# Interleaving VectorE's convolution taps of two chunks, with a third buffer and a later gate load, in an encoder trunk on one Trainium2 core

## The reference, cut to what matters

```python
def conformer_conv_module(h, w_in, b_in, w_dw, b_dw, ln_g, ln_b, w_out, b_out):
    D = h.shape[-1]
    u = h @ w_in + b_in
    u = u[..., :D] * jax.nn.sigmoid(u[..., D:])
    u = lax.conv_general_dilated(
        u, w_dw[:, None, :].astype(u.dtype),
        window_strides=(1,), padding=[(CONV_WIDTH - 1, 0)],
        dimension_numbers=('NWC', 'WIO', 'NWC'), feature_group_count=D) + b_dw
    u = jax.nn.silu(layer_norm(u, ln_g, ln_b))
    return u @ w_out + b_out
# around it:  x = x + g1[:, None, :] * y      (g1 is the gate row that the change loads later)
```

## Time and profile before

| | |
|---|---|
| median of 3 runs | 2036.5 us (2036.23 to 2037.58) |
| the profiled execution's own time | 2046.61 us |
| its span in the profile | 2044.8 us |
| PE busy | 1905.0 us, 93% |
| DVE busy | 1183.9 us, 58% |
| ACT busy | 481.6 us, 24% |
| first tap to last tap on DVE | about 1203 to 1506 us of the span |

### The profile page before, as it was taken

The page is one execution under the profiler, slowest core; times in us unless marked ns, Lnnn a source line. Parts: engine busy times, 40 slices in busy tenths (PEclk is TensorE's granted clock), DMA queues, the critical chain, the costliest instruction groups (busy, mean ns, idle before and its releaser), DMA issues.

```text
span 2044.8 us, 50163 instructions
## 1 busy us (share of the span) xinstructions
PE 1905.0 (93%) x19832; PEld 1150.0 (56%) x19832; DVE 1183.9 (58%) x2132; ACT 481.6 (24%) x1016; POOL 300.8 (15%) x460
## 2 busy tenths in 40 slices
PE   6999999999999978999999699999899589999993
PEld 3444444445666645777777487655445456666661
DVE  3547600368889964333334589999995433333336
ACT  3101000356777840000000140000535000000002
POOL 0001030000000012222222310000001122222233
PEclk8999999799999988999999899999999699999997
DMA  9557520100440088777985913033106899874457
GB/s 395 228 206 281 213 63 0 42 11 11 165 165 11 12 324 314 290 276 255 352 327 202 361 43 109 21 107 107 50 0 235 285 405 407 307 270 175 174 179 265
DMA packets 122589, 390.93 MB, mean 191 GB/s; under 512 B 23776, under 2 KB 44896, under 8 KB 118240
## 3 DMA queue, kind: packets, MB, share of 16 engines
q1 hardware_dynamic: 72720, 303.48, 38.9%
q0 software_dynamic: 21712, 66.46, 9.1%
q10 hardware_dynamic: 28032, 19.17, 3.1%
HBM read 336.80 MB, written 47.49 MB: 188 GB/s over the span
## 4 chain that ended last, share of the span: by engine, by line
PE 76%; DVE 17%; DMA 4%; issue 1%; ACT 1%; SPq 1%; ACTq 0%; POOL 0%; DVEq 0%; POOLq 0%
PE ps L1732 24%; PE ps L1742 12%; DVE kv L1438 11%; PE ps L1558 10%; PE ps L1669 5%; PE ps L1613 5%; PE ps L1627 4%; PE ps L1863 4%; PE ps L1640 4%; PE ps L1652 4%; DMA kv<-in_w_ada 2%; PE ps L1777 1%; PE ps L1535 1%; DMA kv<-in_w_gate_up 1%; DVE pbuf L1085 1%
## 5 line engine op out<-in xcount | busy, mean ns | idle before, releaser
L1732 PE MATMUL ps<-kv,hT 128*32 128x256 f32 x5504 | 387.7, 381 | 5.3 <-DMA kv<-in_w_gate_up 5.3
L1732 PEld LDWEIGHTS ps<-kv,hT 128*32 128x32 f32 x5504 | 226.9, 110 | 82.1 <-issue 8.0
L1438 DVE SCALAR_TENSOR_TENSOR kv<-kv,cols 128x640 f32<-128x640 f32 (+1 forms) x330 | 265.0, 803 | 11.1
L1295 DVE TENSOR_TENSOR hT<-hT,modc 128x256 f32<-128x256 f32 x146 | 62.1, 425 | 302.9 <-PE ps L1732 302.8
L1558 PE MATMUL ps<-hT,ring 128*128 128x512 f32 x512 | 224.3, 599 | 1.2 <-DVE hT L1065 1.2
L805 ACT ACTIVATE hT<-ps 128x128 f32<-128x128 f32 x146 | 40.6, 278 | 747.8 <-PE ps L1732 747.8
L1791 PE MATMUL ps<-hT,ring 128*128 128x320 f32 (+1 forms) x704 | 205.7, 452 | 0.0
L1098 DVE TENSOR_TENSOR_SCAN pbuf<-hT 128x128 f32<-128x128 f32 (+7 forms) x128 | 173.2, 1353 | 47.3 <-ACT hT L747 46.9
L1791 PEld LDWEIGHTS ps<-hT,ring 128*128 128x128 f32 x704 | 132.7, 190 | 69.1 <-issue 2.4
L1558 PEld LDWEIGHTS ps<-hT,ring 128*128 128x128 f32 x512 | 97.6, 192 | 125.8 <-issue 123.9
L1732 PE MATMUL ps<-ring,hT 128*32 128x256 f32 x2560 | 150.8, 388 | 13.0 <-DVE hT L1295 11.4
(11 more groups left out here) (284 smaller groups left out, 2412.3 us busy)
## 6 DMA issues: line engine op xcount, KB each, us to landing
kv<-in_w_gate_up SPq DMA_DIRECT2D x136, 512.0 KB
kv<-in_w_ada SPq DMA_DIRECT2D x20, 2048.0 KB, 7.8
ring<-in_w_gate_up SPq DMA_DIRECT2D x80, 512.0 KB
kv<-in_w_down SPq DMA_DIRECT2D x48, 512.0 KB
ring<-in_w_down SPq DMA_DIRECT2D x40, 512.0 KB
hT<-in_w_gate_up SPq DMA_DIRECT2D x40, 512.0 KB
expert_rows<-hT ACTq DMA_DIRECT2D x584, 32.0 KB
ring<-in_w_in SPq DMA_DIRECT2D x32, 512.0 KB, 6.2
```

The source lines that it names most:

```text
L1438: ins = V.scalar_tensor_tensor(new, old, w_dw_c[:, c, k:k + 1], new, ALU.mult, ALU.add)
L1732: ins = mm(bank(0)[UNIT * q:UNIT * (q + 1), 0:2 * P], xT[:, c, :], wset[s][q // 2][:, 512 * c + 256 * (q % 2):512 * c + 256 * (q % 2) + 25 ...
```

## The change

Two chains of taps run in turn on DVE. Chain 0 does the pieces d = 0, 2, 4, ..., chain 1 the pieces d = 1, 3, 5, ..., and chain 1 begins 18 taps behind. A tap waits for the tap before it in its own chain, which is now two instructions back. Since a piece of each chain is under way and one more may wait to be transposed, there are three buffers, and the third is `bcC`. So the gate row can be loaded only when the last piece in `bcC` (d = 8) has been transposed, and POOL's `load_gate(1, 2)` moves to behind all `make_taps`, with a wait of its own. The positions of DVE's other work are given by a count of taps over all pieces (piece d, tap k was 31 d + k).

```diff
-GATED_AT = {(0, 19): 1, (1, 6): 2, (1, 25): 3, (2, 12): 4, (2, 30): 5, (3, 27): 6, (4, 15): 7, (4, 26): 8, (5, 6): 9,
-            (5, 17): 10, (6, 3): 11, (6, 19): 12, (7, 8): 13, (7, 16): 14, (7, 22): 15}
-KEPT_AT = {(0, 7): FIRST + 1, (0, 17): FIRST + 2}
-MEASURED_AT, SCALED_AT = (7, 15), (7, 18)
-TURNED_AFTER = {2: 0, 4: 1, 6: 2, 7: 3, 8: 4, 10: 5, 12: 6, 14: 7}
+SECOND_CHAIN = 18
+GATED_AT = {17: 1, 37: 2, 56: 3, 74: 4, 92: 5, 120: 6, 139: 7, 150: 8, 161: 9, 172: 10, 189: 11, 203: 12, 225: 13, 233: 14, 239: 15}
+KEPT_AT = {7: FIRST + 1, 16: FIRST + 2}
+MEASURED_AT, SCALED_AT = 252, 255
+TURNED_AFTER = {3: 0, 5: 1, 6: 2, 8: 3, 9: 4, 11: 5, 13: 6, 15: 7}
 SUMMED_AFTER = {5: 0, 10: 1, 11: 2, 12: 3}
...
+        tapped = [cv[:, 0, :], cv[:, 1, :], bcC[:, 0:WIDTH[0]]]
...
             moe(0)
-            load_gate(1, 2)
...
             for n in range(1, len(SUMMED)):
                 pool.wait_ge(taps_summed, n)
                 make_taps(n)
+            pool.wait_ge(conv_turned, TURNED.index(VECTOR[8]) + 1)
+            load_gate(1, 2)
             pool.wait_ge(values_done, 2 * DC)
             pool.dma_start(b_gated, b_out.partition_broadcast(P)).then_inc(bc_loaded, 16)
...
+            last_tap = [0] * len(VECTOR)
+
+            def tap(d, k):
+                h, c = VECTOR[d]
+                new = tapped[d % 3][:, 0:WIDTH[h]]
+                old = u_all[:, c, WIDTH[0] * h + k:WIDTH[0] * h + k + WIDTH[h]]
+                if k == 0:
+                    dve.wait_ge(u_done, DC * h + c + 1)
+                    if d >= 3:
+                        dve.wait_ge(conv_turned, TURNED.index(VECTOR[d - 3]) + 1)
+                    ins = V.tensor_scalar(new, old, w_dw_c[:, c, 0:1], b_dw_c[:, c:c + 1], ALU.mult, ALU.add)
+                else:
+                    dve.wait_ge(dve_step, last_tap[d])
+                    ins = V.scalar_tensor_tensor(new, old, w_dw_c[:, c, k:k + 1], new, ALU.mult, ALU.add)
+                if k == CW - 1:
+                    ins.then_inc(conv_done, 1)
+                    return
+                steps[0] += 1
+                ins.then_inc(dve_step, 1)
+                last_tap[d] = steps[0]
+
             gated(0)
-            for d, (h, c) in enumerate(VECTOR):
...
+            taps = 0
+            for r in range(CW * ((len(VECTOR) + 1) // 2)):
+                for chain, start in enumerate((0, SECOND_CHAIN)):
+                    d, k = 2 * ((r - start) // CW) + chain, (r - start) % CW
+                    if r < start or d >= len(VECTOR):
+                        continue
+                    if taps in KEPT_AT:
+                        norm_keep(2, KEPT_AT[taps])
+                    if taps in GATED_AT:
+                        gated(GATED_AT[taps])
+                    if taps == MEASURED_AT:
                         for g in range(FIRST):
                             statistics(g)
-                    if (d, k) == SCALED_AT:
+                    if taps == SCALED_AT:
                         scales(0, FIRST)
...
+                    tap(d, k)
+                    taps += 1
...
                     d = VECTOR.index((h, c))
                     pe.wait_ge(conv_done, d + 1)
-                    src = cv[:, d % 2, :]
+                    src = tapped[d % 3]
```

More of the change, by code:

```diff
@@ L1416, in scales @@
                                        ln_rstd[:, g:g + n], ALU.mult, ALU.mult).then_inc(ln_scaled, n)
-            gated(0)
-            for d, (h, c) in enumerate(VECTOR):
[L1420 to L1429, removed]
+            last_tap = [0] * len(VECTOR)
@@ L1439, in _ @@
-                    if k < CW - 1:
-                        step(ins)
-                ins.then_inc(conv_done, 1)
+                    tap(d, k)
+                    taps += 1
             def add_output(t):
```

## The result

| | before | changed |
|---|---|---|
| median, 5 runs each | 2036.5 us (2035.2 to 2037.58) | 2046.01 us (2043.54 to 2049.41) |
| ratio | | 1.0043, 95% interval 1.0032 to 1.0054 |
| first tap of DVE to `turn_back(0)` | 1441.99 - 1203.43 = 238.6 | 1449.32 - 1197.54 = 251.8 |
| first tap to the last transpose of the norm that PE waits for | 1582.59 - 1203.43 = 379.2 | 1585.99 - 1197.54 = 388.5 |

The account below looks back on a forecast made before the run. PE was taken as the bound nearly throughout. Later turn_back(0) +13.4, vanished stop at turn_chunk(15) -2.3 and its slow clock -1.5 gave +9.6 us on 2036.5, so 2046.1 us, range 2043 to 2051.

Parts of the forecast that it names:

- the place of the statistics: On DVE, five statistics now stand behind gated(15) and 13 taps, so PE starts turn_back(0) 13.4 us later.
- The second stop and its slow clock: PE's wait for a tap at turn_chunk(15) disappears, -2.3 us, and the slow clock in the matmuls behind it, -1.5 us.
- Cheaper taps turn into waits: Interleaving saves 0.12 us a tap, 37 us of DVE time, which mostly becomes DVE waiting for PE ahead of gated.
- The gate load: POOL's late load of the gate row, behind turn_chunk(10), costs nothing: it lands by some 1495, DVE asks at 1500.
- No cheaper taps: Rival, chance 0.08: DVE's tap steps stay at 0.92 and 0.65 us, as the cited skill page says; +11.6 us, 2048.1.
- Faster: Rival, chance 0.06: statistics end early enough that both PE stops vanish with their slow clocks; 12.4 us gained, 2024.1.
- No change: Rival, chance 0.06: the 17.7 us stop for weights in the second mixture of experts swallows the delay; 2036.5.

Follow-up runs that it names:

- Experiment 2: Kernel before (one chain, two buffers, early gate load), only statistics and scales moved behind gated(15) and 16 taps; 2049.39 us against 2038.21, ratio 1.0051.
- experiment 1: Changed kernel with the five statistics 12 taps earlier, directly behind gated(15); 2039.78 us against 2038.21 for the kernel before, ratio 1.0011.
- experiment 3: Changed kernel with statistics ahead of gated(15) and turn_chunk(7) back behind round 14; 2030.98 us against 2038.21 for the kernel before, ratio 0.9962.
- experiment 5: Kernel of experiment 3 with the gate row loaded later, after turn_chunk(13) instead of turn_chunk(10); 2031.24 us against 2038.07 for the kernel before, ratio 0.9965.
- experiment 6: Kernel of experiment 3 with the gate row loaded only after turn_chunk(15); 2035.79 us, ratio 0.9982 to the kernel before.
- experiment 4: Kernel of experiment 3, but each tap waits for the tap directly before it on DVE; 2042.31 us against 2038.21 for the kernel before, ratio 1.0011.
- experiment 7: Kernel of experiment 3 with gated moved to taps 19 to 247, statistics at 244; 2041.69 us against 2038.07 for the kernel before, ratio 1.0015.

## Why the prediction was right

**The side and the size: the place of the statistics.** The prediction's step was "`gated(15)` and 13 taps, then the five statistics". `turn_back(0)` was forecast 13.4 us later; measured from the first tap it is 13.2 (251.8 against 238.6). Experiment 2 shows this part alone to be enough, and experiments 1 and 3 give the time back by moving it alone, or with one `turn_chunk`.

**The second stop and its slow clock.** Forecast -2.3 and -1.5; measured: no stop, and 13.90 instead of 15.53 us for the matmuls. The sum, 9.6 forecast, is 9.3 in the stage (+13.2 - 2.3 - 1.6) and 9.5 in the medians. That the median came within 0.1 us of the forecast is luck, since the changed kernel's runs alone spread over 6 us.

**Cheaper taps turn into waits.** The steps are 0.80 and 0.53, as read off the rows of instructions that happened not to depend on each other. DVE waits 32.6 us ahead of `gated` (forecast some 30), and its taps are done 296.4 us after the first one began (forecast 1500.1 - 1203.4 = 296.7).

**The gate load.** Free, as forecast: it was issued at 1482.34 and DVE asked at 1493.93 without a wait. Experiments 5 and 6 place the point from which it costs between `turn_chunk(13)` and `turn_chunk(15)`.

**The rivals.** "No cheaper taps" is excluded by the changed kernel's own rows, taps 0.80 us apart, and experiment 4 shows that the relaxed wait does it. The prediction gave the page more strictly than it stands: the same section adds that a next operation that is not held starts earlier, and these taps, 0.88 us long, do start 0.80 us apart. "Faster" named a right condition, statistics that end early against PE's round 15. Experiment 3 has them end 1.4 us ahead of it and gains 7.2 us in the medians and 8.6 in the stage, not 12.4. What this rival left out is what comes between: three taps, `scales`, `gated(15)`, `normalise(0)` and `keep_taps` still hold PE for 3.1 us. "No change" took the 17.7 us of the DMA in the chain for a stop of PE. PE itself waited 5.3 us for these weights in the profile of before and 1.2 to 1.9 in all others, whether the stage took 370.6 or 390.4 us, so there was nothing that could swallow the delay.

**What was missed.** The prediction said of POOL only that its queue was clear. It did not see that the five `make_taps` would take three times as long together (below). That cost nothing in the changed kernel, since `sum_taps` comes later.

## What to carry to other kernels

When an engine beside the bound gets faster, look again at the work that is interleaved with it at fixed counts: left where it was, it turned most of the gain into waits here. Moving the `gated` to later counts was no remedy (experiment 7). The step that the bound engine waits for next, here the statistics, should stand ahead of the last input that this engine takes from it, `gated(15)`, not behind it. Putting a dependence two instructions back instead of one saved 0.12 us a tap, but the order that makes this possible also delays the first of two results. Before an instruction is moved later, all who wait for it are to be listed, the DMA queue and what stands behind its waiting entry included.

## What the runs showed of the hardware that was not expected

**POOL is mostly shut out while DVE's taps run without a gap.** The three long `make_taps` of POOL in order of time in the changed kernel, and on DVE the last tap ahead of a wait and the `gated` behind it:

```profile
1365.80 10.61 POOL L644 TENSOR_TENSOR oT<-maskb,iota_i 128x1024 f32<-128x1024 f32 x1 [69.03 <-PE ps L1845]
1382.16 7.67 POOL L644 TENSOR_TENSOR oT<-maskb,iota_i 128x1024 f32<-128x1024 f32 x1 [5.75 <-PE ps L1845]
1397.98 11.79 POOL L644 TENSOR_TENSOR oT<-maskb,iota_i 128x1024 f32<-128x1024 f32 x1 [8.14 <-PE ps L1845]
```

```profile
1387.20 0.87 DVE L1433 SCALAR_TENSOR_TENSOR kv<-kv,cols 128x640 f32<-128x640 f32 x1
1392.68 0.62 DVE L1400 SCALAR_TENSOR_TENSOR kv<-ps,cols,kv 128x384 f32<-128x384 f32 x1 [4.61 <-PE ps L1808]
```

The second ends at 1389.83, 1.8 us after DVE's tap ended at 1388.07, and the other two also end 1.8 us after a pause of DVE begins. All five take 35.5 us together, 11.9 before, and 10.8 with the chained taps of experiment 4. It goes the other way too. In experiment 7 POOL got in at once at 1384.55, between two taps with no gap, and then a tap took 2.53 us (the same happened once in experiment 1, and `make_taps(3)` took 2.10 us there):

```profile
1384.36 0.87 DVE L1433 SCALAR_TENSOR_TENSOR kv<-kv,cols 128x640 f32<-128x640 f32 x1
1385.15 2.53 DVE L1433 SCALAR_TENSOR_TENSOR bcC<-kv,cols,bcC 128x640 f32<-128x640 f32 x1
```

So the two exclude each other. Experiments 3 and 4 differ only in the wait of the taps, so it is the dependent wait that lets POOL in; that the short gap behind each such tap is how, is argued, not shown. The Trainium skill, "SBUF — State Buffer", section "Who interferes with whom", states the exclusion: DVE and GpSimd share a port pair under an exclusive lock, and a DVE instruction with two inputs in SBUF contends with a GpSimd instruction that reads SBUF. The traces agree: both ways one of the two was held up, by 5 to 9 us on POOL and by 1.7 us on DVE.

**The same stop of PE does not always cost clock.** Stops of 3.06 us at the same place left the granted clock at 1.00 (2.4 GHz) in experiment 3 and at 0.50 (1.2 GHz) in experiment 5, worth 1.4 us. The length of the stop doesn't decide it alone either: 2.32 us at `turn_chunk(15)` before was followed by 0.50, and 2.36 us at `turn_back(0)` in experiment 7 by 1.00. Some of the spread between runs may be of this kind; the runs without a profile don't show it.
